# mLSTM denominators as full rows, two mixers' output tails in one form, and one table for the recurrent gates

## The reference, cut to what matters

```
first block, layer i = 0, 1
  h += 0.5 * swiglu(rms_norm(h))            # 1024 -> 2 x 2816 -> 1024    in_i1, out_i1
  i = 0, recurrent mixer:  y, r = hn @ w_in;  r = causal depthwise conv (4 taps)
      gate_a, gate_x = sigmoid(block-diagonal products of r)
      a = exp(-8 * gate_a * softplus(-lambda))
      b = r * gate_x * sqrt(1 - a^2)
      s_t = a_t * s_(t-1) + b_t;            h += (gelu(y) * s) @ w_out
  i = 1, spatial gating mixer:  u, v = gelu(hn @ w_in);  v = rms_norm(v), mixed over tokens
                                            h += (u * mixed(v)) @ w_out
  h += 0.5 * swiglu(rms_norm(h))                                          in_i2, out_i2

second block, 16 more tokens in front (272 rows), layer l = 0, 1
  z = rms_norm(h) @ w_in;  16 heads of window attention;  4 heads of mLSTM, for each head
      num = P v,  den = row sums of P       (P: masked, gated q k, 272 x 272)
      hm = num / max(|den|, exp(-m));  hm = rms_norm(hm) over the 256 values of the head
  h += concat(attention, hm * gates) @ w_out
```

## Time and profile before

| | us |
|---|---|
| time before, median of 3 runs | 1464.46 (1463.51 to 1465.22) |
| the profiled execution, its own time | 1464.48 |
| its span, first to last instruction | 1462.7 |
| PE busy | 1442.1 (99%) |
| DVE busy | 1100.1 (75%) |
| ACT busy | 822.1 (56%) |
| POOL busy | 283.6 (19%) |

### The profile page before, as it was taken

One profiled execution on the slowest core, in us unless ns is written; L12 is line 12 of the kernel. 1 busy time (PEld: TensorE's weight loads), 2 busy tenths in 40 slices (PEclk: granted clock), 3 DMA queues, 4 the chain that ended last, 5 costly groups with the idle time before them and its releaser, 6 DMA issues.

```text
span 1462.7 us, 27764 instructions
## 1 busy us (share of the span) xinstructions
PE 1442.1 (99%) x9821; PEld 1332.3 (91%) x9821; DVE 1100.1 (75%) x2183; ACT 822.1 (56%) x1492; POOL 283.6 (19%) x348
## 2 busy tenths in 40 slices
PE   8999999899999999999999999999999999999998
PEld 7888899888888888889988888999999999999998
DVE  6777679977766777667777776888769769976983
ACT  6666448566544656445466654556745455576442
POOL 1111113311102111024221112422240125121000
PEclk9999999999999999999999999999999999999999
DMA  6657754556555666555456656543343555434443
GB/s 210 199 187 217 230 169 139 168 184 196 182 189 181 195 188 191 184 190 173 144 185 189 196 163 188 160 129 107 97 116 116 172 141 150 124 94 121 125 134 112
DMA packets 245558, 239.03 MB, mean 163 GB/s; under 512 B 15193, under 2 KB 244425, under 8 KB 245465
## 3 DMA queue, kind: packets, MB, share of 16 engines
q1 hardware_dynamic: 244888, 236.73, 52.8%
q10 hardware_dynamic: 576, 1.05, 0.2%
HBM read 236.70 MB, written 1.05 MB: 163 GB/s over the span
## 4 chain that ended last, share of the span: by engine, by line
PE 90%; DVE 6%; ACT 2%; issue 1%; DMA 1%; POOL 1%; ACTq 0%; DVEq 0%; POOLq 0%
PE bank L614 80%; DVE w_lo L1700 2%; PE bank L971 1%; PE bank L927 1%; PE bank L909 1%; ACT w_hi L1060 1%; PE bank L838 1%; PE bank L848 1%; PE bank L892 1%; PE bank L977 1%; PE bank L987 1%; DMA work<-in_x_dram 1%; PE bank L908 0%; PE bank L928 0%; PE bank L957 0%
## 5 line engine op out<-in xcount | busy, mean ns | idle before, releaser
L614 PE MATMUL bank<-x_both,w_hi 128*128 128x512 f32 (+2 forms) x3552 | 805.4, 332 | 1.5 <-DVE h L1789 1.3
L1700 DVE TENSOR_TENSOR w_lo<-raw,w_hi 128x1024 fp32r<-128x1024 f32 (+1 forms) x456 | 551.5, 1233 | 214.7 <-ACT w_hi L1060 213.7
L1060 ACT CAST w_hi<-raw 128x1024 fp32r<-128x1024 f32 (+1 forms) x456 | 456.9, 1029 | 137.7 <-PE bank L614 125.0
L614 PEld LDWEIGHTS bank<-x_both,w_hi 128*128 128x128 f32 x3552 | 514.7, 189 | 4.7 <-DVE w_lo L1700 1.6
L614 PE MATMUL bank<-x_both,w_lo 128*128 128x256 f32 (+1 forms) x2480 | 496.9, 281 | 0.0
L614 PEld LDWEIGHTS bank<-x_both,w_lo 128*128 128x128 f32 x2480 | 432.4, 189 | 62.6
L614 PE MATMUL bank<-y_both,w_hi 128*128 128x512 f32 (+2 forms) x1472 | 345.7, 337 | 4.9 <-issue 3.5
L614 PEld LDWEIGHTS bank<-y_both,w_lo 128*128 128x128 f32 x1088 | 191.7, 188 | 31.3
L614 PEld LDWEIGHTS bank<-y_both,w_hi 128*128 128x128 f32 x1472 | 212.9, 189 | 5.6 <-issue 3.8
L614 PE MATMUL bank<-y_both,w_lo 128*128 128x256 f32 (+1 forms) x1088 | 215.8, 280 | 0.0
L1585 POOL TENSOR_TENSOR work<-work,rstd 128x256 f32<-128x256 f32 x88 | 63.4, 743 | 416.3 <-ACT work L1107 416.3
(11 more groups left out here) (307 smaller groups left out, 1242.4 us busy)
## 6 DMA issues: line engine op xcount, KB each, us to landing
raw<-in_ffn_w_in_dram SPq DMA_DIRECT2D x176, 512.0 KB, 3.8
raw<-in_w_in_dram SPq DMA_DIRECT2D x100, 512.0 KB, 3.6
raw<-in_ffn_w_out_dram SPq DMA_DIRECT2D x64, 512.0 KB, 4.5
raw<-in_w_out_dram SPq DMA_DIRECT2D x32, 512.0 KB, 4.2
raw<-in_ffn_w_out_dram SPq DMA_DIRECT2D x32, 384.0 KB, 3.3
raw<-in_rec_w_in_dram SPq DMA_DIRECT2D x16, 512.0 KB, 4.3
raw<-in_sg_w_in_dram SPq DMA_DIRECT2D x16, 512.0 KB, 4.4
raw<-in_rec_w_out_dram SPq DMA_DIRECT2D x8, 512.0 KB, 3.4
```

What stands on the lines that cost most here:

```text
L614: i_ = mm(accs[m][:, cols], w[:, s, j, m * P:(m + 1) * P], moving, start=begin and g == 0, stop=final)
L1060: nc.scalar.copy(w_hi[:, s, 0:n, :], raw[:, s, 0:n, :]).then_inc(hi_made, 1)
L1700: TT(w_lo[:, s, 0:n, :], raw[:, s, 0:n, :], w_hi[:, s, 0:n, :].bitcast(fp32), SUB).then_inc(lo_made, 1)
```

## The change

**mLSTM.** The row sums of P and the sums of squares are made by products with a matrix of ones, so that they stand as a row in every partition (272 columns). The stages' waits and the visits stay. Stage 1 gains a broadcast of the row `g_row[:, 5]`; ACT squares the sums, DVE takes the maximum (stage 1) and adds the sum of squares (stage 2), ACT takes the root (`head_root`), and DVE the reciprocal of the whole row (`inverse_root`). Stage 3 has no product any more. `rsqrt`, the diagonals and three small transposes (L874) in each layer go.

**Recurrent mixer.** The sigmoids become tanh of half the argument, with the factors put into the decay's scale and bias, and `one_more` adds one to the input gate. ACT makes the first tap of half the convolution, two convolutions stand one unit later on DVE, the last gate products one half unit earlier on PE. POOL squares the decay before it multiplies by the gate.

**Output tails.** `sg_out` takes the form of `rec_out`. In `rec_out` PE adds the residual by a product with the identity, ACT copies the tile to h. In both, ACT squares the chunks and POOL only adds. The sum over partitions for the next norm stands half a unit later, and the second pair of tiles of `in02` and `in12` goes to banks 6 and 7.

```diff
-EIGHT_TILES = ("rec_out",)
+EIGHT_TILES = ("rec_out", "sg_out")
+PE_ADDS = ("rec_out",)
...
+FIRST_BANK = {2 * PHASES[_n][1] + 2 + _m: 6 + _m for _n in ("in02", "in12") for _m in range(2)}
...
-GATES_AT = (None, 5, 7, 9)
-GATES_MID = {4: 0}
+GATES_AT = (None, 5, 7)
+GATES_MID = {4: 0, 9: 3}
...
+            def add_residual(T):
+                mm(bank[BANK_OF[T]][:, 0:SEQ], ident, h[:, T - T_OUT[T], META:L], start=True, stop=False)
...
-                             mid=sum_of_x if n == 0 and j > p else None)
-                    if j == 0 and n:
+                             mid=sum_of_x if n == 0 and j > p else (lambda: norm_sum(n, META)) if n in (2, 5) and j > p else None)
+                    if j == 0 and n not in (0, 2, 5):
                         norm_sum(n, META)
...
-                        for j, (ja, jb) in enumerate(LT):
-                            for t, (a, b) in enumerate(LT[:j + 1]):
-                                at = MOFF[t] + ja - a
-                                pj = m_pt[:, at:at + jb - ja] if j < 2 else wide_pt(at)
-                                i_ = mm(bank[4][0:max(jb - ja, FULL), 400 + j:401 + j], pj, ones[:, 0:1], start=t == 0,
-                                        stop=t == j)
-                        i_.then_inc(m_num, 1)
+                        for t, (a, b) in enumerate(LT):
+                            mm(bank[4][:, a:L], ones[:, :], m_pt[:, MOFF[t]:MOFF[t] + L - a], start=t == 0, stop=t == 2)
+                        mm(bank[5][:, 0:L], ident[:, hd:hd + 1].broadcast_to((P, P)), g_row[:, 5, :], start=True,
+                           stop=True).then_inc(m_num, 1)
...
+                        for w in range(2):
+                            i_ = mm(bank[5][:, 0:L], ones[:, :], n_sq[:, w, :], start=w == 0, stop=w == 1)
                         i_.then_inc(m_ms, 1)
-                    if stage == 3:
-                        pe.wait_ge(m_diag, n + 1)
-                        if hd < M_H - 1:
-                            pe.wait_ge(m_exp_new, n + 2)
-                        for j, (a, b) in enumerate(LT):
-                            sum_of = ones[:, :] if j < 2 else tri[:, TAIL - 1:TAIL].broadcast_to((P, P))
-                            i_ = mm(bank[4][:, a:b], sum_of, diag[:, j, 0:b - a], start=True, stop=True)
-                        i_.then_inc(m_bb, 1)
...
+                        activation(d_max, bank[4][:, 0:L], ACT.Square).then_inc(m_dsq, 1)
+                    if stage == 2:
+                        root_table()
+                        roots_due.append(n)
+                def head_root():
+                    while roots_due:
+                        n = roots_due.pop()
+                        act.wait_ge(ms_read, n + 1)
...
+                        activation(d_root, d_max, ACT.Sqrt, scale=1.0 / 16).then_inc(m_root, 1)
...
+                            nc.scalar.copy(h[:, 2 * p + m, META:L], bank[BANK_OF[T]][:, 0:SEQ]).then_inc(tile_read, 1)
...
+                            activation(squared[c % 2][:, META:L], h[:, c, META:L], ACT.Square).then_inc(h_squared, 1)
...
-                        activation(dst[:, c, :], bank[4 + c % 4][:, k * SEQ:(k + 1) * SEQ], ACT.Sigmoid,
-                                   bias=pcol(b, c)).then_inc(gates_sig, 1)
+                        activation(dst[:, c, :], bank[4 + c % 4][:, k * SEQ:(k + 1) * SEQ], ACT.Tanh, scale=0.5,
+                                   bias=decay[:, b, c:c + 1]).then_inc(gates_sig, 1)
...
+                dve.wait_ge(m_root, n + 1)
+                V.reciprocal(s_b, d_root).then_inc(m_sb, 1)
...
                                 kind, n = steps[0]
                                 do[kind](n)
+                                if n[0]:
+                                    inverse_root(M_H * l + n[0] - 1)
                                 later = [steps[0]]
                                 steps = steps[1:]
                             if gate_later:
```

More of the change, by code:

```diff
@@ L586, in unit @@
                 s = U % RING
-                accs = [bank[BANK_OF.get(2 * pair + m, (2 * pair + m) % 4)] for m in range(tiles)]
+                accs = [bank[tile_bank(2 * pair + m, off)] for m in range(tiles)]
                 def bank_free(m):
@@ L604, in unit @@
                     begin, end = first and j == 0, last and j == n - 1
+                    residual = 2 * pair in T_OUT
                     if both:
@@ L613, in unit @@
                                 bank_free(m)
-                            i_ = mm(accs[m][:, cols], w[:, s, j, m * P:(m + 1) * P], moving, start=begin and g == 0,
-                                    stop=final)
+                                if residual and BANK_OF[2 * pair + m] < 4:
+                                    add_residual(2 * pair + m)
+                            i_ = mm(accs[m][:, cols], w[:, s, j, m * P:(m + 1) * P], moving,
+                                    start=begin and g == 0 and not residual, stop=final)
                             if final and m == 0 and tiles == 2:
@@ L666, in out_phase @@
                 if name in EIGHT_TILES:
+                    if name in PE_ADDS:
+                        pe.wait_ge(gates_sig, 2 * NC8)
+                        for t in range(4):
+                            add_residual(2 * pb + t)
                     for j in range(2):
@@ L1220, in mult @@
                     r = rec_p[:, b:b + 4, 0:SEQ]
-                    activation(r, r, ACT.Sqrt).then_inc(mult_new, 1)
+                    activation(r, r, ACT.Sqrt, scale=0.25).then_inc(mult_new, 1)
             def gelu(c, n):
@@ L1291, in _ @@
                     activation(sg_u[:, c, :], sg_u[:, c, :], ACT.Gelu_apprx_tanh).then_inc(sg_gelu, 1)
-            for c in range(4, NC8):
-                act.wait_ge(act_new, NC8 + c + 1)
-                split_x(y_hi, c, SEQ, sg_s[:, c, :])
-            out_phase("sg_out", lambda c: pcol("ffn2_norm", NC8 + c))
+            out_phase("sg_out", lambda c: pcol("ffn2_norm", NC8 + c), before=lambda: upper2(range(6, 8)))
             in_phase("in12", 5)
@@ L1576, in h_squares @@
                     link(TT(mv[:, :, 0:META], h[:, :, 0:META], h[:, :, 0:META], MUL))
+                if name in EIGHT_TILES:
+                    b = EIGHT_TILES.index(name)
+                    for c in range(1, NC8):
+                        pool.wait_ge(h_squared, NC8 * b + c + 1)
+                        if c > 1:
+                            pool.wait_ge(sq_added, 6 * b + c - 1)
+                        part = sq[:, T0:L] if c == 1 else sumsq[:, T0:L]
+                        TT(sumsq[:, T0:L], part, squared[c % 2][:, T0:L], ADD).then_inc(
+                            sq_added if c < NC8 - 1 else sq_done, 1)
+                    return
                 squares(lambda c: h[:, c, T0:L], lambda c: pool.wait_ge(tile_read, 2 * pb + c + 1), T0, sq_done,
@@ L1785, in out_phase @@
                     if name in EIGHT_TILES:
-                        for m in range(2):
+                        for m in range(2) if name not in PE_ADDS else ():
                             c = 2 * p + m
@@ L2007, in _, with second_half2 @@
             for p in (2, 3):
-                ahead(pb + p)
-                if p == 3:
-                    dve.wait_ge(sg_read, NC8)
-                    outputs2(range(4))
+                for j, (U, _, _) in enumerate(units_of(pb + p)):
+                    split_w(U + LEAD)
+                    if (p, j) == (2, 0):
+                        dve.wait_ge(sg_read, NC8)
+                        outputs2(range(4))
+                    if (p, j) == (3, 0):
+                        lower2(range(4))
+                        outputs2(range(4, 6))
                 for m in range(2):
                     scaled(pb + p, m, sg_u[:, 2 * p + m, :], SEQ, META)
-            outputs2(range(4, 6))
-            outputs2(range(6, 8))
-            out_phase("sg_out", lambda c: pcol("ffn2_norm", NC8 + c), SPLITS["x_in12"], half=1.0)
+            def second_half2():
+                lower2(range(4, 6))
+                outputs2(range(6, 8))
+                lower2(range(6, 8))
+            out_phase("sg_out", lambda c: pcol("ffn2_norm", NC8 + c), SPLITS["x_in12"], half=1.0, before=second_half2)
             in_phase("in12", 3, 5, SPLITS["y_out12"])
```

171 lines of the change are left out of this document (104 added, 67 removed).

## The result

The changed kernel took **1468.09 us** (median of 7 runs, 1466.22 to 1470.46) beside 1463.86 (7 runs, 1463.39 to 1465.22) for the kernel before: ratio 1.0027, 95% interval [1.0018, 1.0037]. That is 1.8 us over the 1466.3 that I forecast and within the range of 1456.5 to 1470.5. The profiled execution took 1466.89 us, with a span of 1465.1.

The account below looks back on a forecast made before the run. PE, busy for 99% of the span, was taken to bound the kernel. Terms +4.9 (mLSTM), -2.7 (recurrent mixer) and -0.4 (gating mixer) gave +1.8 us on 1464.48: 1466.3 us, with 8 in 10 between 1456.5 and 1470.5.

Parts of the forecast that it names:

- mLSTM: Forecast term for the mLSTM: PE's work -4.6 us and the reciprocal's waits +9.5 us, together +4.9 us.
- recurrent mixer: Forecast term: stops gone -6.8 us, residual products +3.4, later norm sum +0.7 at `in02`, together -2.7 us.
- gating mixer: Forecast term: a stop of 1.4 us goes and one of 1.0 us comes at `in12`, together -0.4 us.
- The reciprocal's stall: mLSTM, ahead of stage 1: the reciprocal delays `taken`, PE waits three times 1.44 and three times 1.74 us, +9.5 us.
- The rival in which DVE does not hold PE: mLSTM: the wait before the mask would hold the reciprocal, so PE is not stalled; 1456.8 us, chance 0.23.
- PE's work in the mLSTM: Changed products of the three stages -0.52 us a head, -4.2 for eight; fewer small transposes -0.4; together -4.6 us.
- the seven stops that the other mixers lose: PE's six stops in the recurrent mixer and one in the gating mixer: 6.8 and 1.4 us to win, 0.14 added each.
- no other wait grows, since the splits are three units ahead: mLSTM, units behind the waiting PE: they follow late, but no wait beyond those ahead of stage 1 grows.
- My fear that the chain would not get shorter: Rival, recurrent mixer: DVE's own work bounds the chain, so the first three stops stay; 1468.2 us, chance 0.11.
- only 4.6 us are left: PE stops for 1.0 us: At `in12`, with the norm's sum half a unit later: 4.6 us remain for a 5.6 us chain, PE stops 1.0 us.
- tails become slower: Rival, both output phases: late tile pairs move squares, sum and root; up to 3 us each, +4.3, 1470.6 us, chance 0.13.
- the rival in which a switch costs more than its load: At the two roots a table switch costs as much as a load again, 1.3 us each; 1468.9 us, chance 0.05.

Follow-up runs that it names:

- e3: The changed kernel with the mLSTM of before, recurrent mixer and tails staying changed: 1461.01 us, ratio 0.9979 to before.
- e11: The changed kernel run again with no edit: 1467.28 us (8 runs), ratio 1.0029 to before.
- e10: The recurrent mixer's part of the change alone, mLSTM and gating mixer in their forms of before: 1459.85 us, ratio 0.9972 to before.
- e8: The change, gating mixer included, with root ahead of ACT's split, reciprocal ahead of the mask and `taken` ahead of DVE's split: 1461.89 us, ratio 0.9985 to before.
- e7: The change with root ahead of ACT's split, reciprocal ahead of the mask, `taken` ahead of DVE's split, and the gating mixer of before: 1460.66 us.
- e6: The change with sigmoid in place of tanh in the recurrent gates, so that tables switch again: 1470.68 us, ratio 1.0048 to before.
- e5: The change with the residual of `rec_out` added by DVE again in place of PE's eight products: 1469.03 us, ratio 1.0044 to before.
- e4: The changed kernel with the gating mixer's output phase in its form of before: 1465.67 us, ratio 1.0020 to before.
- e1: The changed kernel with DVE's reciprocal of 272 columns replaced by a copy of the same row: 1458.88 us, ratio 0.9965 to before.
- e2: The changed kernel with `taken` ahead of the weight split in its unit, nothing left out: 1462.07 us, ratio 0.9985 to before.

## Why the prediction was right, and where it was not

The time came out within 2 us and the range, 14 us wide, held. But by the traces each of the three terms was further off (0.9, 0.8 and 0.9 us) than their sum (0.6), the recurrent mixer with the opposite sign: that the sum came so close is in part luck.

| part | predicted | in the traces | by runs |
|---|---|---|---|
| mLSTM | +4.9 | +5.8 | +7.0 (change against e3; 6.3 with e11) |
| recurrent mixer | -2.7 | -3.5 | -4.5 (e10 against before; 1.0 of it POOL's addition) |
| gating mixer | -0.4 | +0.5 | +1.2 (e8 against e7; 1.0 of it the same addition) |

- **The reciprocal's stall**: waits of 1.44 and 1.74 us, three of each, were predicted; they are 1.42 and 1.72, by the mechanism and at the place that I named. Here the rows of before were enough: a price from the earlier trace rows, the order in DVE's loop, and the slack of the earlier trace rows. The rival in which DVE does not hold PE would have needed the reciprocal ahead of the mask; e7 shows what it takes, an edit on two engines.
- **PE's work in the mLSTM**: from one stage 1 to the next it was 18.20 us before (1074.83 to the earlier trace rows's 1093.03) and is 19.20 after (1090.41 to 1109.61), with 1.42 of idle. I wrote -0.52 for a head. The products before the stop start at 1088.58, two of 0.125 us, so the next was due at 1088.83 and came at 1090.41: a stop takes 1.58, and the head's work fell by 0.58. The work was right to 0.06.
- **What I left out there**: that 0.16 us of restart. I counted 0.14 for each of the seven stops that the other mixers lose, and not for the six that the mLSTM gains: 1.0 us. And at the end of layer 1 one more wait comes, 0.4 us for `w_lo` ("no other wait grows, since the splits are three units ahead" failed there). These two, 1.4 us, less the 0.5 that the heads' work fell by more than I wrote (8 x 0.06), are the gap between 4.9 and 5.8.
- **What no single trace of before could give**: the clock behind a stop (e11). It is a likely source of the last 1.2 us between the traces and the runs, but this was not shown, and in e11 some 0.8 of them are not there.
- **Recurrent mixer**: the stops went. The first of them hangs on the one table, as I wrote (e6). Others stay away only because PE adds the residual, which I had counted as a cost alone: that the products also keep DVE's tail from being late (e5), I had not seen. Their cost was right: the first four take 1.55 us (252.38 to 253.93 on PE's timeline of after), the others 0.43 each, 3.25 in all against 3.4. The wait at `in02` is 0.4 us in place of 0.7. And 0.4 us were won ahead of the first stop (from the sum to 252.88 it was 47.99 us before, to the same product at 252.14 it is 47.60), for which I had no term. My fear that the chain would not get shorter did not come true.
- **Gating mixer**: the step that failed is the 1.0 us in "only 4.6 us are left: PE stops for 1.0 us", and with it the sign of the term. The 4.6 was right: the sum starts at 732.89 and the fifth unit was due at 737.51. But the chain behind the sum became longer than the 5.6 us that I took over from before, the unit came at 739.12, and a second wait, at the first product of `in12`, was not in the sum. PE's timeline of after:
```profile
725.79 0.74 PE L639 MATMUL bank<-x_both,w_hi 128*128 128x512 f32 x2 [0.45 <-DVE h L1867]
...
732.89 0.59 PE L665 MATMUL bank<-sumsq,ones 128*128 128x256 f32 x2
...
739.12 0.84 PE L639 MATMUL bank<-x_both,w_hi 128*128 128x512 f32 x2 [1.44 <-DVE work L1824]
```
  Behind both is DVE, where my bounds named ACT or POOL. DVE's timeline of after in the tail:
```profile
723.55 1.76 DVE L1776 TENSOR_TENSOR w_lo<-raw,w_hi 128x1024 fp32r<-128x1024 f32 x1
725.23 0.74 DVE L1867 SCALAR_TENSOR_TENSOR h<-bank,h 128x256 f32<-128x256 f32 x2
726.30 0.48 DVE L1789 SCALAR_TENSOR_TENSOR x_both<-h,par,x_both 128x256 fp32r<-128x256 f32 x1 [0.33 <-ACT x_both L1079]
727.01 0.67 DVE L1789 SCALAR_TENSOR_TENSOR x_both<-h,par,x_both 128x256 fp32r<-128x256 f32 x1 [0.22 <-ACT x_both L1079]
727.60 1.76 DVE L1776 TENSOR_TENSOR w_lo<-raw,w_hi 128x1024 fp32r<-128x1024 f32 x1
```
  A tile pair takes DVE 4.05 us, from one split to the next, where PE makes one in 2.9: 1.76 for a split that takes 1.2 elsewhere (an addition of POOL, 0.74 at 723.49, lies beside it), and 0.55 of waiting for ACT in between. So the third pair empties its banks late, which is the 0.45 us. The last pair is later still, and ACT waits for it. ACT's timeline of after:
```profile
729.73 0.51 ACT L1079 ACTIVATE x_both<-h,par 128x256 fp32r<-128x256 f32 x1 [2.52 <-DVE h L1867]
...
733.16 1.28 ACT L1092 ACT_TABLE_LOAD   x1
```
  The load for the root now starts 0.27 us behind the sum, where before it started 0.26 ahead of it; that makes the chain 0.5 us longer and the stop 1.44 in place of 1.0. At `in02` the same load is over 0.4 us before its sum comes (284.32 and 1.28; the sum is at 285.98), and the stop there is 0.42. This is the rival "tails become slower", with DVE in place of ACT as its engine and at a fifth of its price (0.9 of 4.3 us). By runs it costs 1.2 us against e7, but 1.0 of that is POOL's addition (e4), for which the kernel before waits too.
- **The root's table**: the rival in which a switch costs more than its load did not come true. ACT's timeline of after, at the first head's root:
```profile
1079.09 1.28 ACT L1092 ACT_TABLE_LOAD   x1
1080.38 0.20 ACT L1092 ACTIVATE root_of_eps<-epsc 128x1 f32<-128x1 f32 x1
```
  The next activation starts 0.01 us behind the load, and e1, which keeps all the loads, loses the stall but for 2.4 us.

## What to carry to other kernels

When a long instruction is put into an in-order queue, its cost here was its length less the idle time that it could reach, counted at the next deadline behind it; moving one instruction past another may be worth more than the instruction itself (e2: 6 us from the place of a split). Where a part is to be judged by runs, run it with and without the other parts: here errors of 2.1 and 1.6 us stood against one of 1.8 in the sum, and most of the gating mixer's loss by runs was an order between two engines 200 us away. A stop of the matrix engine cost its idle time, a restart of some 0.15 us, and in some executions its clock, so six short stops were dearer than they look in one profile.

## What the runs showed that I had not expected

- The granted clock fell to 0.50 behind stops of 1.72 us (e11) and, in e6's trace, behind the one of 2.13 us at 256.38 (0.50 from 258 to 260), and in other executions it did not fall behind the same stops: 1.00 in the result's profile from 1380 on, and 1.00 behind the stop of 2.20 us in the earlier trace rows.
- One addition of POOL took 0.78 or 1.73 us by whether it started 0.04 us ahead of DVE's split or 0.32 behind it.
- A reciprocal of 128x272 on DVE takes 1.83 us, a copy of the same tile 0.28.
